# Compression pages copied position by position before their products, with the page numbers held in registers

## What is computed

```
def compress(rows, pos, w1, w2):
    n, l = rows.shape[:2]
    blk = rows.reshape(n, l // CMP_BLOCK, CMP_BLOCK, 2, N_KV_HEADS, HEAD_DIM) + pos[None, None, :, :, None, :]
    hid = jax.nn.silu(jnp.einsum('ncbkgd,kbdh->nckgh', blk, w1))
    return jnp.einsum('nckgh,khd->nckgd', hid, w2)
...
comp_p = compress(pad_rows(cmp_p, SEL_BLOCK), cmp_pos, cmp_w1, cmp_w2)
past_cmp = cache_cmp_kv[page_table].reshape(...)
full_cmp = pad_rows(jnp.concatenate([past_cmp, cmp_s], axis=1), SEL_BLOCK)
comp_s = compress(full_cmp, cmp_pos, cmp_w1, cmp_w2)
```

## Time and profile before

| | us |
|---|---|
| median of 3 runs | 1902.67 (1894.96 to 1903.57) |
| the profiled execution | 1892.15 |
| its span | 1890.4 |
| PE busy | 1676.7 (89%), 11980 instructions |
| DVE busy | 878.4 (46%) |
| ACT busy | 578.5 (31%) |
| POOL busy | 480.9 (25%) |
| mean granted clock of PE | 0.945 of 2.4 GHz |

### The profile page before, as it was taken

One profiled execution on the slowest core, in us unless ns is written; L12 is line 12 of the kernel. 1 busy time (PEld: TensorE's weight loads), 2 busy tenths in 40 slices (PEclk: granted clock), 3 DMA queues, 4 the chain that ended last, 5 costly groups with the idle time before them and its releaser, 6 DMA issues.

```text
span 1890.4 us, 32215 instructions
## 1 busy us (share of the span) xinstructions
PE 1676.7 (89%) x11980; PEld 1456.1 (77%) x11980; DVE 878.4 (46%) x2316; ACT 578.5 (31%) x1289; POOL 480.9 (25%) x307
## 2 busy tenths in 40 slices
PE   3899999996978988889999998999999999883795
PEld 1688888885968876878788887888878888761695
DVE  1544455554234231455655555564555645662223
ACT  2433343341113220123343333333433333340001
POOL 0223212227331242451011111110110110276130
PEclk8899999997999989889999999999999999996998
DMA  9132233225131333101121211110010100225312
GB/s 344 34 115 96 96 117 124 96 91 168 56 123 33 150 87 103 55 12 32 26 54 37 57 32 47 55 37 23 21 37 22 36 27 17 74 78 167 113 34 101
DMA packets 77771, 143.01 MB, mean 76 GB/s; under 512 B 18834, under 2 KB 49586, under 8 KB 77458
## 3 DMA queue, kind: packets, MB, share of 16 engines
q1 hardware_dynamic: 68266, 130.73, 21.5%
q0 software_dynamic: 3456, 7.08, 1.3%
q10 hardware_dynamic: 5904, 3.21, 0.6%
HBM read 126.86 MB, written 19.35 MB: 77 GB/s over the span
## 4 chain that ended last, share of the span: by engine, by line
PE 76%; DVE 7%; issue 6%; ACT 4%; DMA 2%; POOL 2%; POOLq 1%; ACTq 1%; SPq 0%; DVEq 0%
PE PS L813 14%; PE PS L815 13%; PE PS L814 13%; PE PS L1025 8%; PE PS L1012 8%; PE PS L992 4%; PE PS L1122 3%; PE PS L993 3%; ACT XT L1207 1%; PE PS L1002 1%; ACT HT_r L1210 1%; PE PS L844 1%; PE PS L957 1%; POOLq L539 1%; PE PS L1021 1%
## 5 line engine op out<-in xcount | busy, mean ns | idle before, releaser
L813 PE MATMUL PS<-HT_r,WR_r 128*128 128x344 f32 x1368 | 464.4, 339 | 56.1 <-DVE XT_r L1407 25.8
L815 PE MATMUL PS<-HT_r,WR_r 128*128 128x344 f32 x1368 | 446.1, 326 | 0.0
L814 PE MATMUL PS<-XT_r,WR_r 128*128 128x344 f32 x1368 | 445.6, 326 | 0.0
L551 POOL TENSOR_TENSOR WR_r<-WR,ONE 128x1024 fp32r<-128x1024 f32 x65 | 126.9, 1952 | 1122.4 <-DMA WR<-w_b 674.2
L813 PEld LDWEIGHTS PS<-HT_r,WR_r 128*128 128x128 f32 x1368 | 266.0, 194 | 63.4 <-DVE WR L1464 28.9
L1286 ACT ACTIVATE PB<-PB,NM 128x257 f32<-128x257 f32 (+9 forms) x384 | 248.8, 650 | 192.1 <-DVE NM L1565 191.5
L814 PEld LDWEIGHTS PS<-XT_r,WR_r 128*128 128x128 f32 x1368 | 265.9, 194 | 0.4
L815 PEld LDWEIGHTS PS<-HT_r,WR_r 128*128 128x128 f32 x1368 | 265.1, 194 | 0.0
L1025 PE MATMUL PS<-PT,VT 128*64 128x128 f32 x2592 | 223.3, 288 | 8.6 <-DVE PT L1578 4.3
L1012 PE MATMUL PS<-CST,PB 128*128 128x128 f32 (+1 forms) x1360 | 225.4, 285 | 1.9 <-ACT PB L1282 1.3
L1578 DVE COPY PT<-PS 128x256 f32<-128x256 f32 (+2 forms) x192 | 121.4, 633 | 184.7 <-PE PS L1012 184.2
(11 more groups left out here) (252 smaller groups left out, 2313.6 us busy)
## 6 DMA issues: line engine op xcount, KB each, us to landing
WR<-w_ada SPq DMA_DIRECT2D x64, 512.0 KB, 5.2
WR<-w_b SPq DMA_DIRECT2D x32, 512.0 KB, 3.4
WR<-w_a SPq DMA_DIRECT2D x17, 512.0 KB, 5.0
STR<-scratch SPq DMA_DIRECT2D x128, 48.0 KB, 1.9
XT<-x SPq DMA_DIRECT2D x8, 516.0 KB, 15.0
HT<-x SPq DMA_DIRECT2D x8, 516.0 KB, 4.5
x_mid<-HT SPq DMA_DIRECT2D x8, 516.0 KB, 6.4
HT<-x_mid SPq DMA_DIRECT2D x8, 516.0 KB, 4.4
```

The source lines that it names most:

```text
L551: pool.tensor_tensor(high_r, raw, ONE[:, 0:1].unsqueeze(2).to_broadcast([P, NC, P]), ALU.mult).then_inc(sem("w_split"), 1)
L813: pe.matmul(out, hw[:, k, :], high, start=(k == 0), stop=False)
L814: pe.matmul(out, hw[:, k, :], low, start=False, stop=False)
L815: return pe.matmul(out, lw[:, k, :], high, start=False, stop=(k == NC - 1))
```

## The change

Each page buffer is no longer read by PE. ACT and DVE first copy it into a second place, `cm_columns`, in which the 192 columns of one b stand side by side; there is one such place, not two, made of three tiles that are free here: KD for b 0 to 9, PB for 10 to 14, QT for 15. ACT copies b 0 to 7 in one instruction of 1536 columns. DVE copies b 8 to 15 in three, of 384, 960 and 192 columns. Reads are now 16 columns apart in these copies, and side by side in the products. PE waits for ACT's copy (`cm_turn_a`), runs 8 products, raises `cm_half`, waits for DVE's copy (`cm_turn_d`), and runs the other 8. ACT's copy for the next step waits for `cm_half`, DVE's for `cm_mm`. A page buffer is free as soon as both copies of it are made. `pages_there` holds the waits for the transfers that PE had.

The page numbers of the stage are read once: 22 by SP, 22 by POOL and 20 by ACT (`compression_numbers`), at the three places named above, and the page loads become plain sequences of transfers without a loop. On POOL the wait for the end of the stage (`cm_mm`, 6) now stands ahead of `split_keys("sel", 1)`, which writes to KD.

```diff
+        def share(third_, part):
+            return ((0, 8), (8, 8), (16, 8))[part] if third_ < 2 else ((0, 6), (6, 6), (12, 4))[part]
+        def compression_numbers(eng, part):
+            eng.wait_ge(sem("pages_in"), 16)
+            at = [CM_PAGES * third_ + share(third_, part)[0] + j for third_ in range(3) for j in range(share(third_, part)[1])]
+            return {i: eng.value_load(PGT[0:1, i:i + 1], min_val=0, max_val=79) for i in at}
-        def compression_pages(eng, part, st):
+        def compression_pages(eng, part, st, numbers):
...
             if st >= 2:
-                eng.wait_ge(sem("cm_mm"), st - 1)
-            first, n = ((0, 8), (8, 8), (16, 8))[part] if third_ < 2 else ((0, 6), (6, 6), (12, 4))[part]
-            with eng.Fori(0, n // 2) as i:
-                pages = [eng.value_load(PGT[0:1, bass.ds(i * 2 + third_ * CM_PAGES + first + j, 1)], min_val=0, max_val=79) for j in range(2)]
-                for j, page in enumerate(pages):
-                    eng.dma_start(CM[st % 2][:, bass.ds(i * 2 * P + (first + j) * P, P)],
-                                  t["cmp_pool"][bass.ds(page, 1), k].rearrange("o p n -> (o p) n"))\
-                       .then_inc(sem(f"cm_full{part}{st % 2}"), 16)
+                eng.wait_ge(sem("cm_turn_a"), st - 1)
+                eng.wait_ge(sem("cm_turn_d"), st - 1)
+            first, n = share(third_, part)
+            for j in range(first, first + n):
+                eng.dma_start(CM[st % 2][:, j * P:(j + 1) * P],
+                              t["cmp_pool"][bass.ds(numbers[CM_PAGES * third_ + j], 1), k].rearrange("o p n -> (o p) n"))\
+                   .then_inc(sem(f"cm_full{part}{st % 2}"), 16)
+        def cm_columns(b0, n):
+            if b0 < 10:
+                return KDs[:, 0:2, :].rearrange("p a n -> p (a n)")[:, b0 * 192:(b0 + n) * 192]
+            return PB[:, 2, (b0 - 10) * 192:(b0 - 10 + n) * 192] if b0 < 15 else QTf[:, 0:192]
+        def turned_pages(eng, copy, st, b0, n):
+            pages = CM[st % 2][:, :].rearrange("p (n x b) -> p b n x", x=8, b=16)[:, b0:b0 + n]
+            return copy(cm_columns(b0, n).rearrange("p (b n x) -> p b n x", b=n, x=8), pages)
...
             splits(N_Q0 + 6, N_AO)
+            cm_numbers = compression_numbers(pool, 1)
             pool.wait_ge(sem("fill_mm"), FM_A)
...
+            pool.wait_ge(sem("cm_mm"), 6)
             split_keys("sel", 1, 4, N_B + 1)
-            pool.wait_ge(sem("cm_mm"), 6)
...
                         strip(it + 2, s, SEQ - 2 * P, SEQ, 512 * (it % 2), f"strip{s}{it % 2}")
+            cm_numbers = compression_numbers(sp, 0)
...
+                pe.wait_ge(sem("cm_turn_a"), st + 1)
                 if st >= 2:
                     pe.wait_ge(sem("hid"), st - 1)
                 for b in range(16):
-                    last = pe.matmul(PS[:, st % 2, 0:CM_PAGES * 8], W1[:, k, b, :], CM[st % 2][:, b::16],
+                    if b == 8:
+                        last.then_inc(sem("cm_half"), 1)
+                        pe.wait_ge(sem("cm_turn_d"), st + 1)
+                    last = pe.matmul(PS[:, st % 2, 0:CM_PAGES * 8], W1[:, k, b, :], cm_columns(b, 1),
                                      start=(b == 0), stop=(b == 15))
...
             decode("a", WIN_A, 2)
+            cm_numbers = compression_numbers(act, 2)
             norm("b", lambda c: act.wait_ge(sem("op_ev"), 3 * c + 3))
...
+            def turned(st):
+                pages_there(act, st)
+                if st:
+                    act.wait_ge(sem("cm_half"), st)
+                turned_pages(act, lambda out, in_: act.activation(out, in_, ACT.Copy), st, 0, 8).then_inc(sem("cm_turn_a"), 1)
+            act.wait_ge(sem("kv_stored"), 96)
+            turned(0)
             act.wait_ge(sem("pc_ev"), 2)
             for st in range(6):
+                if st < 4:
+                    compression_pages(act, 2, st + 2, cm_numbers)
+                if st < 5:
+                    turned(st + 1)
                 act.wait_ge(sem("cm_mm"), st + 1)
...
-                if st < 4:
-                    compression_pages(act, 2, st + 2)
...
+            def turned(st):
+                if st % 3 == 2:
+                    dve.wait_ge(sem("cm_turn_a"), st - 1)
...
+                pages_there(dve, st)
+                if st:
+                    dve.wait_ge(sem("cm_mm"), st)
+                for b0, n in ((8, 2), (10, 5), (15, 1)):
+                    ins = turned_pages(dve, dve.tensor_copy, st, b0, n)
+                ins.then_inc(sem("cm_turn_d"), 1)
+            dve.wait_ge(sem("kv_stored"), 96)
+            turned(0)
             for st in range(6):
                 k, third_ = divmod(st, 3)
+                if st < 5:
+                    turned(st + 1)
                 dve.wait_ge(sem("hid_tanh"), st + 1)
```

More of the change, by code:

```diff
@@ L516, in compression_pages, with pages_there @@
             if st >= 2:
-                eng.wait_ge(sem("cm_mm"), st - 1)
-            first, n = ((0, 8), (8, 8), (16, 8))[part] if third_ < 2 else ((0, 6), (6, 6), (12, 4))[part]
-            with eng.Fori(0, n // 2) as i:
-                pages = [eng.value_load(PGT[0:1, bass.ds(i * 2 + third_ * CM_PAGES + first + j, 1)], min_val=0, max_val=79) for j in range(2)]
-                for j, page in enumerate(pages):
-                    eng.dma_start(CM[st % 2][:, bass.ds(i * 2 * P + (first + j) * P, P)],
-                                  t["cmp_pool"][bass.ds(page, 1), k].rearrange("o p n -> (o p) n"))\
-                       .then_inc(sem(f"cm_full{part}{st % 2}"), 16)
+                eng.wait_ge(sem("cm_turn_a"), st - 1)
[12 more added lines that the diff above has]
+            return copy(cm_columns(b0, n).rearrange("p (b n x) -> p b n x", b=n, x=8), pages)
+        def pages_there(eng, st):
+            for part in range(3):
+                loads_ = sum(8 if s % 3 < 2 else (6, 6, 4)[part] for s in range(st % 2, st + 1, 2))
+                eng.wait_ge(sem(f"cm_full{part}{st % 2}"), 16 * loads_)
+            if st % 3 == 2:
+                eng.wait_ge(sem("cm_own"), st // 3 + 1)
         EARLY_PAGES = 24
@@ L590, in _ @@
             for st in range(6):
-                compression_pages(pool, 1, st)
+                compression_pages(pool, 1, st, cm_numbers)
             splits(N_B0 + 1, N_B + 1)
             pool.wait_ge(sem("kv_stored"), 96)
+            pool.wait_ge(sem("cm_mm"), 6)
             split_keys("sel", 1, 4, N_B + 1)
-            pool.wait_ge(sem("cm_mm"), 6)
             split_keys("win", 0, 8, N_B + 1)
@@ L749, in _ @@
             for st in range(6):
-                compression_pages(sp, 0, st)
+                compression_pages(sp, 0, st, cm_numbers)
             sp.wait_ge(sem("gl_ev"), 2)
@@ L1113, in _ @@
                 k, third_ = divmod(st, 3)
-                for part in range(3):
-                    loads_ = sum(8 if s % 3 < 2 else (6, 6, 4)[part] for s in range(st % 2, st + 1, 2))
-                    pe.wait_ge(sem(f"cm_full{part}{st % 2}"), 16 * loads_)
-                if third_ == 2:
-                    pe.wait_ge(sem("cm_own"), k + 1)
+                pe.wait_ge(sem("cm_turn_a"), st + 1)
                 if st >= 2:
@@ L1323, in _ @@
             high_keys("sel")
-            compression_pages(act, 2, 0)
+            compression_pages(act, 2, 0, cm_numbers)
             act.wait_ge(sem("lin_mm"), L_GL + 1)
             act.activation(third(GL[0:3 * H, :]), PS[0:3 * H, 0:3, 0:THIRD], ACT.Tanh, scale=0.5).then_inc(sem("gl_tanh"), 1)
-            compression_pages(act, 2, 1)
+            compression_pages(act, 2, 1, cm_numbers)
+            def turned(st):
[5 more added lines that the diff above has]
+            turned(0)
             act.wait_ge(sem("pc_ev"), 2)
             for st in range(6):
+                if st < 4:
+                    compression_pages(act, 2, st + 2, cm_numbers)
+                if st < 5:
+                    turned(st + 1)
                 act.wait_ge(sem("cm_mm"), st + 1)
@@ L1752, in _ @@
             dve.wait_ge(sem("pc_ev"), 2)
-            for st in range(6):
-                k, third_ = divmod(st, 3)
-                if third_ == 2:
-                    if st >= 2:
-                        dve.wait_ge(sem("cm_mm"), st - 1)
+            def turned(st):
+                k = st // 3
+                if st % 3 == 2:
+                    dve.wait_ge(sem("cm_turn_a"), st - 1)
                     pages = CM[st % 2][:, 16 * P:24 * P].rearrange("p (j g x) -> p j g x", j=8, g=2)
@@ L1764, in _ @@
                     ins.then_inc(sem("cm_own"), 1)
+                pages_there(dve, st)
[6 more added lines that the diff above has]
+            turned(0)
+            for st in range(6):
+                k, third_ = divmod(st, 3)
+                if st < 5:
+                    turned(st + 1)
                 dve.wait_ge(sem("hid_tanh"), st + 1)
```

1 line of the change is left out of this document (removed).

## The result

Beside runs of the kernel before on the same chip, the changed kernel took 1873.93 us (median of 4 runs, 1870.12 to 1880.24), the kernel before 1899.72 (4 runs, 1894.96 to 1903.57). The medians are 25.8 us apart. The measured ratio is 0.9881, with a 95% interval from 0.9857 to 0.9905; it is not the quotient of the medians (0.9864) and stands for 22.6 us. Timed again later, six runs gave 1876.80 us against 1895.64 for the kernel before, 18.8 us less, ratio 0.9888 (0.9866 to 0.9911). The forecast was 1879.0 us, a gain of 23.7.

A forecast was written before the change was run, and what follows sets the result against it. The prediction took PE as the bound almost everywhere, its strided products limited by reads, not clock. Terms -32.4 + 5.1 + 2.4 - 4.4 + 3.6 + 2.0 = -23.7 us, from 1902.67 to 1879.0 us; range 1867 to 1893 us.

The forecast's parts named there:

- 1 products: PE's first products in the six steps: 0.164 us each with side-by-side columns instead of 0.333, -32.4 us.
- 2 clock: PE idle ahead of steps 0, 4 and 5: low clock at their heads costs 1.7 us each, +5.1 us.
- 4 start of step 0: Ahead of step 0: ACT's page transfers and copy let PE start at 684.7 instead of 682.28 us, +2.4 us.
- 6 gaps: Between steps: copies hidden in steps 0 to 2, gaps behind steps 3 and 4 grow to 4.0 us, +3.6 us.
- 7 POOL's splits: POOL's splits move to the end of step 4; three copies and reorder lose 2.0 each, 2.0 returned, +2.0 us.
- 8 page numbers: Page number reads on SP, ACT and POOL: L1046 starts 5.1 us late, absorbed by later waits, 0 us.
- everything cheap: Rival, chance 0.12: copies take 1.26 and 1.6 us and do not meet POOL; -28.2 us, 1874.5 us.
- The change does not do what it says: Rival, chance 0.05: stride is not what makes PE's products slow, product and clock terms are nothing; +3.6, 1906.3 us.
- the rival at 1889.6 us: Clock rival, chance 0.15: each gap costs the whole next step, 15.75 instead of 5.1 us; -13.0 us.
- The middle: Copy length on ACT and DVE: 2.2 us each, between plain-copy or nearest-row speed and PE's strided speed.
- rival at 1882.2 us: Rival, chance 0.13: copies run at the strided speed, lengthening the start of step 0 and the gaps; -20.4 us.
- Starved: Rival, chance 0.05: DVE's copies behind POOL's page issues and splits take 13 us in each step; +57, 1936 us.

The follow-up runs named there:

- e8_side_by_side: The kernel before, page numbers in loops, no copies, first products reading 192 side-by-side (wrong) columns; stage 74.9 us against 96.9.
- e2_copies: The changed kernel with page numbers read in loops again instead of kept in registers; 1889.08 us, ratio 0.9954 to the kernel before.
- e3_even: The changed kernel with VectorE's copy of five positions cut into one of four and one of one; 1861.38 us in one run.
- e6_act_first: e3_even with ScalarE issuing its page loads of step 1 behind its copy for step 0; 1859.04 us in one run, stage 60.4 us.
- e12_act_first_again: The kernel of e6_act_first profiled and timed again in the last comparison on one chip; stage 69.8 us.
- e5_fill: e3_even with unused TensorE products, 12 ahead of step 0 and 8 behind the products of steps 3 and 4; step 0 took 5.2 us.
- e10_fill_one: e12_act_first_again with 8 unused TensorE products behind the products of step 4; six times from 1855.63 to 1878.20 us, stage 62.3 us.

## Why the prediction was right

Its time and its stage agree: forecast -23.7 us, measured -25.8 between the medians, -22.6 by the ratio and -23.0 in the profiled stage. Term by term for that execution, in us:

```
term                     forecast  measured  from
1 products                  -32.4     -31.3  6 x (5.40 - 10.62)
2 clock                      +5.1      +5.1  7.50, 7.09, 6.68 less 5.40 each
4 start of step 0            +2.4      +2.5  8.1 against 5.6
5 prompt's own pages         -4.4      -4.4  no wait for L1801
6 gaps                       +3.6      +3.9  4.15 against 2.2, twice
7 POOL's splits              +2.0      +1.3  8.56 - 4.15, less 3.1 at the tail
8 page numbers                0         0
sum                         -23.7     -22.9
```

The mechanism is right in the terms 1, 4, 5 and 6, and in these the second execution of the changed kernel is close to the first (start 8.2 us, gap ahead of step 4 4.4 us). That the whole sum falls within 1 us is luck in part. In the second execution the clock cost 8.1 us instead of 5.1 and the meeting with POOL 5.2 instead of 4.4, so that the stage took 78.2 us, 18.7 less than before. Nor does the time decide between the cases: 1873.93 us lies nearer to "everything cheap" (1874.5) than to the forecast (1879.0). The trace rules that case out, as the copies took 2.83 and 2.4 us rather than 1.6 and 1.26 and did meet POOL's splits.

**Products.** One takes 0.169 us, not 0.164; that small size is 1 us over 192. The reads were the cause, as e8_side_by_side shows with no copies at all. "The change does not do what it says" falls.

**Clock.** The windows are low at the head of steps 0, 4 and 5 and at full level in steps 1 to 3. That each costs the whole step, the rival at 1889.6 us, falls. The forecast took 1.7 us for each; they were 2.1, 1.7 and 1.3, and in the second execution 3.1, 2.7 and 2.4. In the kernels with copies, steps 1 to 3 took 5.40 us in every execution but that of e2_copies, where TensorE waited ahead of steps 2 and 3. So a low clock at a head goes with an idle stretch. The reverse does not hold: behind a gap of 3.4 us step 4 took 5.41 us in e3_even and e6_act_first and 7.09 in e12_act_first_again. Filler removed the loss in step 0 (e5_fill) and step 5 (e10_fill_one), in one execution each, which supports the idle stretch as the cause and does not prove it.

**The copies.** The middle was the wrong value for ScalarE: 2.83 us is the strided end. For VectorE 2.2 us was about right in sum (2.4), and wrong in kind. I took one cost per column; from 1 to 2 and from 2 to 4 positions a further column cost half of PE's, and the piece of 5 ran at PE's. The sentence that took "the middle, as one row has the engine and the other the reads" averaged two things of which one or the other applies, by the shape of the piece. The rule of the Trainium skill ("SBUF — State Buffer", "Door 1: The DMA port swizzle") that I set against the change holds for ScalarE (2.83 against 1.48 us with contiguous reads) and for VectorE (0.51 against 0.36 us for two positions; the 1.80 against 0.65 of the piece of five also holds what its shape costs). Its rival at 1882.2 us did not come, as the longer copy on ScalarE is hidden from step 1 on and cost only 0.6 us at the start of step 0, of which its earlier begin (5.1 us behind the gate product instead of 5.6) gave back 0.5.

**Start of step 0.** Right in its chain: e6_act_first takes the page issues out of it and PE starts 4.1 us sooner.

**Gaps.** 4.15 us, forecast 4.0. What sets them is VectorE's copies: 0.7 us less with the even piece, 1.1 with contiguous reads.

**POOL.** The place was right, the kind of cost was not. I let the gap lose 4.0 us, 2.0 for the copies and 2.0 for the reorder. In the profiled execution it was 4.4, and in the second one of the same kernel 9.52 - 4.37 = 5.2 us. Over all kernels with copies it was anything from 0 to 7.1 us (3.7 against 10.8), by whether VectorE ends ahead of POOL's start. The tail gave back 3.1 us where I had 2.0, since I had left out L1770, which the same meeting had made 0.9 us longer. "Starved" at every turn (1936 us) falls: only the last turn met POOL's splits. In the changed kernel no copy lay beside a page issue; in e2_copies some did and kept their length (0.48 to 0.54, 1.75 to 1.84 and 0.31 to 0.34 us).

Nor are all copies held. In the second execution of the changed kernel a split of POOL lies at 735.75 to 737.64 us. The copy of two positions that starts beside it takes 1.86 us instead of 0.50 and ends 0.35 us behind it, and the piece of five runs through the next split at its usual length:

```profile
736.13 1.86 DVE L543 COPY KD<-MT 128x384 f32<-128x384 f32 x1 [6.38 <-PE PS L1149]
737.92 1.75 DVE L543 COPY PB<-MT 128x960 f32<-128x960 f32 x1
```

```profile
737.71 2.50 POOL L579 TENSOR_TENSOR WR_r<-WR,WR_r 128x1024 fp32r<-128x1024 f32 x1
```

**Page numbers.** Right: 4.1 us late where 5.1 was forecast, and absorbed. What I did not see is that the registers, here costed at nothing, carry some 14 us of the result, because ScalarE's page loads stand ahead of its copies. The forecast had them in, since I worked with the register issues from the start, but the term "8" looked only for their cost.

**Base.** Counting from the median rather than from the profiled 1892.15 us was right: that execution had a short stretch behind the stage. From 1892.15 the forecast would have been 1868.5, below all four runs. But the median of three was high: the kernel before took 1899.72 us in four runs and 1895.64 to 1897.49 in the later timings. From these the same -23.7 would give 1872 to 1876 us, beside the 1873.93 and 1876.80 measured.

## What to carry to other kernels

Where a product's time does not change with the granted clock, look at the distance between the columns that it reads; a copy that lays them side by side pays even at strided speed, if it runs on engines that wait. Cut such copies and time each shape: one position more, five instead of four, took VectorE from 0.82 to 1.80 us here. When a stage gets shorter, look up which transfers and splits now fall into its gaps, and give the forecast two values there rather than a mean.

## What was unexpected in the hardware

A copy of 192 columns from a stride of 64 bytes took 0.33 us on VectorE, 384 columns 0.51, 768 columns 0.82, and 960 columns 1.80 us; with contiguous reads 960 took 0.65 us. ScalarE's 1536 columns took 2.83 and 1.48 us. Two VectorE copies (768 and 192 columns) that met POOL's splits went from 1.03 to 2.75 us, and one of 192 columns from 0.31 to 2.50, as if it waited for one whole split (1.9 to 2.4 us). The copy of 960 columns, the slow one, was not held: 1.75 us with a split beside it. Beside POOL's page issues the copies kept their length. And one kernel's stage took 60.4 or 69.8 us, 7.1 of it by a margin of some 2 us between two engines.
